# Gathering the V rows of a mixture of experts by token instead of by slot, one tile later

## The chip, the cores and the metric

One core of a Trainium2 chip (trn2) runs the whole program. The metric is the device time of one execution in microseconds (us). The kernel before takes 4674.15 us, the median of three runs (4666.22 to 4674.29).

## What is computed

One decoder layer for 1024 prompt tokens and 64 sample tokens, all in float32. After the mixers (gated linear attention and sliding-window attention) comes the part that this case is about: each token picks 128 of 16384 single-neuron experts, 16 for each of 8 heads, takes the dot product of its normalized state with each expert's row of U, and adds up the experts' rows of V, weighted.

```python
    top_s, sel = lax.top_k(cand, PEER_TOPK)
    idx = jnp.take_along_axis(cand_idx, sel, axis=-1)
    g = jax.nn.softmax(top_s, axis=-1)
...
        ub = jnp.take(u, ib, axis=0)
        act = jax.nn.gelu(jnp.einsum('pd,ped->pe', xb, ub), approximate=False)
        vb = jnp.take(v, ib, axis=0)
        return jnp.einsum('pe,ped->pd', gb * act, vb)
...
    h = x + merged @ w_out
    h = h + peer_ffn(rmsnorm(h, norm_ffn), peer_w_q, peer_keys1, peer_keys2, peer_u, peer_v)
```

A row of U or V has 1024 numbers, 4 KB. For 1088 tokens with 128 experts each, two rows per expert, that is 1.14 GB of rows fetched by index.

## The kernel before

Three stages run one after another: `project_stage` (the projections), `mix_stage` (the two mixers and their merge) and `peer_stage` (W_out, the norm, the experts, the final norm). The change is in the last, which takes the span from about 1424 us on.

`peer_stage` works in tiles of 128 tokens, one token on each partition: tiles 0 to 7 hold the prompt, tile `LAST` = 8 the 64 sample tokens. In a tile run 8 heads; a tile and a head make a unit. Tile 0 and tile `LAST` are written out, tiles 1 to 7 run in a hardware loop. Each engine has its own program:

- POOL (L1424 to L1461) fetches. One gather is one indirect DMA: it brings, for one slot k of one head, 128 rows of 4 KB, one for each token's partition. In a unit it issues 16 gathers of U for this head and, in turn with them, 16 of V for the head before. U and V rows land in rings of 8 buffers each. Before each gather it waits until its buffer was used (`u_used`, `v_used`). In tile `LAST` the 64 tokens stand on the partitions twice, and each gather brings two slots (`expert_pair`), so that a head takes 8 gathers.
- DVE (L1553 to L1709) does for each U row buffer one dot product with the normalized state (`u_dots`, L1625), then `select` for the unit two further on (L1587: the top 16 of 128 keys twice, then of 256 sums, and the experts' numbers), then `weights` of its own unit. At heads 4 and 5 it adds the residual of the next tile (`residual`), before head 6 it takes part in its norm (`norm`), after the dots of head 7 it copies the next tile's state (`take`).
- ACT (L1464 to L1550) applies Gelu to a head's dots and Exp to its scores, and makes for each slot a 128 x 128 matrix with the 128 tokens' weights on its diagonal (`diagonals`, L1493, a ring of 8).
- PE (L1712 to L1816) multiplies each diagonal with the slot's V rows, in two halves of 512 columns, into one accumulator `o_ps` of 128 x 1024, over all heads of the tile (`v_sum`, L1768). `carry` starts that sum from the residual. Between the V sums stand the queries and scores of the unit two further on, W_out of the next tile, and at head 6 the transposes of the next tile's state. A float32 matmul shows in the profile as two instructions.
- SP loads x and the mixers' result for each tile and stores the output.

`g` of the reference is `e_top` times `e_rec`; `expert` holds the numbers of the rows. The waits are on counting semaphores; an engine runs its program in order and stands at each wait.

Of the kernel before, what the change touches and what calls it, by code (L numbers as in the profile page):

```python
# [22 lines left out]
U32 = mybir.dt.uint32  # L23
# [1207 lines left out]
def peer_stage(nc, sem, x_dram, m_dram, wo_dram, wq_dram, keys_dram, u_dram, v_dram, g_ffn_dram, g_final_dram, y_dram):  # L1231
# [6 lines left out]
    U_RING, V_RING = 8, 8  # L1238
    IDX = 4
    WQ_PARTS = 2  # L1240
    DIAGS = 8
    W_OUT = {2: (0,), 3: (1,), 4: (2, 3)}
    RESIDUAL = (4, 5)
    with ExitStack() as ctx:
# [17 lines left out]


        room = sb("e_room", [P, D])
        xn_next = y = room
        mT = room[:, :].rearrange("p (k n) -> p k n", k=KT)
        xn = sb("e_xn", [P, D])
# [14 lines left out]
        picked = sb("e_picked", [P, 2, TOPK])  # L1282
        expert = sb("e_expert", [P, IDX, TOPK], U32)
        expert_pair = sb("e_expert_pair", [P, IDX, TOPK // 2], U32)
        neg_best = sb("e_neg_best", [P, IDX])
# [3 lines left out]
        dots = sb("e_dots", [P, 2, TOPK])  # L1289
        gelus = sb("e_gelus", [P, 2, TOPK])  # L1290
        weight = sb("e_weight", [P, 2, TOPK])
        diag = sb("e_diag", [P, DIAGS, P])
# [17 lines left out]
        h_used = sem("e_h_used")  # L1310
        moved = sem("e_moved")
# [11 lines left out]
        paired = sem("e_paired")  # L1323
# [7 lines left out]
        diag_ready = sem("e_diag_ready")  # L1331
        acc_ready = sem("e_acc_ready")
# [6 lines left out]
        tick = sem("tick")  # L1339
        pstep = sem("e_pstep")  # L1340
        block = ctx.enter_context(nc.Block())
        LAST = TILES

        def rows(t):
            return NSAMP if isinstance(t, int) and t == LAST else P

        def slots(t, h=0):

            return TOPK // 2 if isinstance(t, int) and t == LAST and h >= 0 else TOPK

        def slots_before(unit):

            if isinstance(unit, int) and unit > LAST * HEADS:
                return LAST * HEADS * TOPK + (unit - LAST * HEADS) * (TOPK // 2)
            return unit * TOPK

        def rounds(unit, k, ring):

            if isinstance(unit, int):
                return slots_before(unit) // ring + k // ring + 1  # L1360
            return unit * (TOPK // ring) + k // ring + 1

        @block.sync
        def _(sp):

            def load_merge(t):
                wait_alone(sp, moved, t, tick)
                wait_alone(sp, xnT_ps, 2 * t, tick)
# [8 lines left out]
            def store(t):  # L1377
                wait_alone(sp, y_ready, t + 1, tick)
                sp.dma_start(y_dram[bass.ds(t * P, rows(t)), :], y[0:rows(t), :]).then_inc(y_stored, 16)
# [536 lines left out]
```

## Time and profile before

| | |
|---|---|
| median of the runs | 4674.15 us (4666.22 to 4674.29) |
| span of the profiled execution | 4664.4 us |
| PE busy | 3850.8 us, 83% of the span |
| DVE busy | 2478.5 us, 53% |
| POOL busy | 2471.3 us, 53% |
| ACT busy | 1078.6 us, 23% |
| gathered by POOL's queue | 1143.22 MB |
| mean granted clock of TensorE | 0.910 |

The span runs from the first to the last instruction of one execution. A busy time counts the union of an engine's instructions; an engine that is busy for a large share need not be the one that the others wait for. POOL's busy time on a gather is the time in which it makes the transfer's descriptors; the data land some microseconds later. "issue" is time in which an engine waited for nothing that the profile shows.

### The profile page before, as it was taken

Reading aid. Unit: us, or ns where it says so; the run is one execution under the profiler, and the core shown is the slowest. Engines: PE = TensorE matmul, PEld = TensorE weight load, DVE = VectorE, ACT = ScalarE, POOL = GpSimd, SP = SyncE. Lnnn points to the kernel's source line nnn. Section 1 sums busy time; section 2 is a strip of 40 time slices with the busy share of each in tenths; the row PEclk is TensorE's granted clock in tenths of the full one; section 3 lists DMA queues with packets and bytes.
Section 4 is the critical chain, followed back from the end, with each engine's and each line's share of the span. In section 5 each row is a group of like instructions: output and inputs, shape, how many; then the busy total and the mean of one; then the engine's idle time right before and its main releaser. Section 6 shows DMA issues by size and latency. Waiting matters only on the chain.

```text
span 4664.4 us, 46976 instructions
## 1 busy us (share of the span) xinstructions
PE 3850.8 (83%) x13480; PEld 2174.6 (47%) x13480; DVE 2478.5 (53%) x6136; ACT 1078.6 (23%) x2482; POOL 2471.3 (53%) x2212
## 2 busy tenths in 40 slices
PE   8999997899884878787887787787788787878787
PEld 7888885555442334343343343343334343434332
DVE  3111004655434666666666666666666666666665
ACT  4221113333210212212222212222222121212221
POOL 0000000000002777777777777777777777777766
PEclk9999997999967999898999898989898999898989
DMA  3222214221136999999999999999999999999988
GB/s 135 89 85 99 77 41 155 75 65 46 53 100 252 369 379 350 385 368 362 368 375 371 367 382 363 360 373 361 358 389 352 363 374 364 346 374 358 361 322 309
DMA packets 393667, 1291.38 MB, mean 277 GB/s; under 512 B 48440, under 2 KB 84536, under 8 KB 391368
## 3 DMA queue, kind: packets, MB, share of 16 engines
q0 software_dynamic: 313920, 1143.22, 65.1%
q1 hardware_dynamic: 61080, 116.93, 7.4%
q10 hardware_dynamic: 18432, 28.42, 1.7%
q8 instruction: 109, 1.79, 0.2%
q14 instruction: 126, 1.03, 0.1%
HBM read 1243.87 MB, written 45.71 MB: 276 GB/s over the span
## 4 chain that ended last, share of the span: by engine, by line
PE 30%; DVE 14%; DMA 12%; issue 8%; POOL 3%; ACT 2%; POOLq 0%; ACTq 0%; DVEq 0%; SPq 0%
PE e_o_ps L1776 24%; DMA e_u_rows<-in_u,e_expert 8%; PE e_q_ps L1744 4%; DMA e_v_rows<-in_v,e_expert 3%; POOL e_v_rows L1429 2%; POOL e_u_rows L1429 1%; DVE e_pairs L1583 1%; DVE e_pairs L1608 1%; DVE e_top_idx L1585 1%; DVE e_top_idx L1582 1%; DVE e_pairs L1612 1%; DVE e_picked L1614 1%; DVE e_top_val L1584 1%; DVE e_pos L1585 1%; PE e_w_ps L1731 1%
## 5 line engine op out<-in xcount | busy, mean ns | idle before, releaser
L1776 PE MATMUL e_o_ps<-e_v_rows,e_diag 128*128 128x512 f32 (+1 forms) x4352 | 2061.4, 626 | 380.7 <-ACT e_diag L1499 289.3
L1631 DVE CUSTOM_DVE_ANT_0 e_u_rows<-e_u_rows,e_xn 128x1024 f32<-128x1024 f32 x1088 | 1300.6, 1223 | 1058.0 <-DMA e_u_rows<-in_u,e_expert 974.5
L1776 PEld LDWEIGHTS e_o_ps<-e_v_rows,e_diag 128*128 128x128 f32 (+1 forms) x4352 | 828.9, 197 | 1464.2 <-issue 1375.3
L1429 POOL DMA_INDIRECT e_v_rows<-in_v,e_expert x1024 | 1177.2, 1150 | 351.1 <-issue 250.8
L1429 POOL DMA_INDIRECT e_u_rows<-in_u,e_expert x1024 | 1114.3, 1088 | 376.4 <-issue 268.7
L1499 ACT ACTIVATE e_diag<-e_ident,e_weight 128x128 f32<-128x128 f32 x1024 | 361.9, 395 | 872.9 <-PE e_o_ps L1776 869.4
L1744 PEld LDWEIGHTS e_q_ps<-e_xnT,e_wq 128*128 128x128 f32 x2304 | 307.7, 209 | 117.9 <-issue 109.2
L1744 PE MATMUL e_q_ps<-e_xnT,e_wq 128*128 128x128 f32 x2304 | 314.4, 294 | 40.3 <-issue 34.0
L578 POOL TENSOR_TENSOR p_gate<-p_gate,gn 128x1024 f32<-128x1024 f32 x8 | 18.9, 2357 | 448.9 <-DMA p_gate<-z_tok 448.9
L373 PE MATMUL j_m<-j_wh,j_xh 128*128 128x512 f32 (+1 forms) x648 | 248.0, 383 | 4.5 <-DVE j_wl L309 2.5
L374 PE MATMUL j_m<-j_wl,j_xh 128*128 128x512 f32 (+1 forms) x648 | 246.2, 380 | 0.0
L375 PE MATMUL j_m<-j_wh,j_xl 128*128 128x512 f32 (+1 forms) x648 | 245.9, 380 | 0.0
L730 POOL MEMSET m_ident<- 128x128 f32 x1 | 0.2, 204 | 457.1 <-POOLq L115 457.1
L309 DVE TENSOR_TENSOR j_wl<-j_w,j_wh 128x4096 fp32r<-128x4096 f32 (+1 forms) x13 | 55.5, 4271 | 339.1 <-ACT j_wh L223 339.1
L1491 ACT ACTIVATE e_gelus<-e_dots 128x16 f32<-128x16 f32 (+1 forms) x72 | 15.5, 215 | 952.2 <-DVE e_dots L1631 952.2
L229 ACT ACTIVATE j_stage<-j_m 128x512 f32<-128x512 f32 (+1 forms) x132 | 70.5, 534 | 506.9 <-PE j_m L375 506.8
L1484 ACT ACTIVATE e_e_top<-e_best,e_neg_best 128x16 f32<-128x16 f32 x72 | 22.1, 307 | 599.7 <-DVE e_expert L1615 599.7
L373 PE MATMUL j_m<-j_xh,j_wh 128*128 128x512 f32 (+1 forms) x432 | 152.3, 353 | 2.2 <-ACT j_stage L229 2.2
L374 PE MATMUL j_m<-j_xl,j_wh 128*128 128x512 f32 (+1 forms) x432 | 152.2, 352 | 0.0
L375 PE MATMUL j_m<-j_xh,j_wl 128*128 128x512 f32 (+1 forms) x432 | 151.7, 352 | 0.0
L1731 PE MATMUL e_w_ps<-e_wo,e_room 128*128 128x512 f32 x288 | 130.1, 601 | 16.0 <-DMA e_room<-merged 16.0
L373 PEld LDWEIGHTS j_m<-j_wh,j_xh 128*128 128x128 f32 x648 | 123.2, 190 | 29.4 <-DVE j_wl L309 2.9
(255 smaller groups left out, 3930.1 us busy)
## 6 DMA issues: line engine op xcount, KB each, us to landing
j_w<-in_w_big SPq DMA_DIRECT2D x12, 2048.0 KB, 8.1
z_tok<-j_stage ACTq DMA_DIRECT2D x64, 256.0 KB, 2.0
e_u_rows<-in_u,e_expert POOLq DMA_INDIRECT x1024, 6.3
e_v_rows<-in_v,e_expert POOLq DMA_INDIRECT x1024, 6.3
z_feat<-j_stage ACTq DMA_DIRECT2D x32, 256.0 KB, 2.0
e_wq<-in_wq SPq DMA_DIRECT2D x2, 4096.0 KB, 24.0
e_room<-merged SPq DMA_DIRECT2D x9, 512.0 KB, 6.6
e_h_next<-in_x SPq DMA_DIRECT2D x9, 512.0 KB, 9.3
```

The costliest lines, as they stand in the source:

```text
L229: act.activation(stage[0:n, slot, 0:width], m_ps[slot][0:n, 0:width], func).then_inc(staged, 1)
L309: dve.tensor_tensor(wl[:, s, 0:width], w[:, 0:width], wh[:, s, 0:width].bitcast(F32), ALU.subtract).then_inc(wl_ready, 1)
L373: pe.matmul(out, lh, rh, start=(k == 0), stop=False)
L374: pe.matmul(out, lh, rl, start=False, stop=False)
L375: last = pe.matmul(out, ll, rh, start=False, stop=(k == KT - 1))
L1429: pool.indirect_dma_start(ring[:, k % size, :], None, table, bass.IndirectOffsetOnAxis(ap=index[:, h % IDX, k:k + 1], axis=0)).then_inc(go ...
L1499: act.activation(diag[:, k % DIAGS, 0:eye.shape[1]], eye[:, :], ACT.Copy, scale=weight[:, h % 2, k:k + 1]).then_inc(diag_ready, 1)
L1585: chain.step(dve.max_index(indices[:, 8:16], values[:, 8:16], rest))
L1631: dve.tensor_tensor_reduce(u_rows[:, k % U_RING, :], u_rows[:, k % U_RING, :], xn[:, :], 1.0, 0.0, ALU.mult, ALU.add, dots[:, h % 2, k:k + ...
L1731: last = pe.matmul(w_ps[:, c * BANK:(c + 1) * BANK], mT[:, k, :], wo[:, k, c * BANK:(c + 1) * BANK], start=(k == 0), stop=(k == KT - 1))
L1744: last = pe.matmul(q_ps[:, half, :], wq[:, k, j * P:(j + 1) * P], xnT[:, k, :], start=(k == 0), stop=(k == KT - 1))
L1776: last = pe.matmul(o_ps[0:n, c * BANK:(c + 1) * BANK], diag[:, k % DIAGS, 0:n], v_rows[:, k % V_RING, c * BANK:(c + 1) * BANK], start=Fals ...
```

## The change

The V rows are fetched the other way round. A gather now brings, for one token, the rows of all its 128 experts, one on each partition. For that the experts' numbers of a whole tile are collected in `expert_f`, transposed by PE and copied by DVE (`turn_experts`), which is possible only when all 8 heads of the tile are selected; so the V rows of tile t are fetched during tile t + 1, a gather of U and one of V in turn as before. In tile `LAST` two V gathers follow each U gather, and after it come the 64 V gathers of tile `LAST` itself.

The weights of a tile are collected too (`dots`, `gate`, `weights`), transposed (`turn_weights`) and put by ACT, four tokens at a time, into a column of a window that is zero elsewhere (`place`). PE takes a token's V rows with 32 columns of that window, so that the token's sum falls on its own partition within a group of 32; the tokens j, 32 + j, 64 + j and 96 + j go to the four column groups (`quad`). A quad frees its four buffers at once.

The residual no longer goes through PE; SP keeps it in DRAM (`h_dram`), loads it again two tiles later, and DVE adds the sum to it (`out_sum`). The ring of U has 7 buffers instead of 8, the state is kept for two tiles instead of being copied, the hardware loops of this stage are written out, and before the stage all semaphores of the stages before it are cleared behind a barrier (`reset`).

```diff
-    U_RING, V_RING = 8, 8
...
+    U_RING, V_RING = 7, 8
     IDX = 4
     WQ_PARTS = 2
-    DIAGS = 8
+    QUADS = 32
+    WIN = 64
     W_OUT = {2: (0,), 3: (1,), 4: (2, 3)}
     RESIDUAL = (4, 5)
...
+        xn = sb("e_xn", [P, 2, D])
...
+        window = sb("e_window", [P, 2, 4, WIN])
...
+        def lanes(t):
+            return 4 if t < LAST else 2
+        def v_at(t, j, g):
+            return t * P + lanes(t) * j + g
...
+            def load_h(t):
+                sp.wait_ge(wo_done, 2 * min(t + 3, LAST + 1))
+                wait(sp, y_stored, 16 * t)
+                sp.wait_ge(h_stored, 16 * (t + 1))
+                sp.dma_start(room[0:rows(t), :], h_dram[t, 0:rows(t), :]).then_inc(h_back, 16)
...
+            def u_gather(t, h, k):
+                i = u_at(t, h, k)
...
+            def v_gather(t, n):
+                j, g = divmod(n, lanes(t))
+                i = v_at(t, j, g)
+                wait(pool, v_used, quad_of(i - V_RING) + 1)
+                token = 32 * g + j
+                pool.indirect_dma_start(v_rows[:, i % V_RING, :], None, v_dram,
+                                        bass.IndirectOffsetOnAxis(ap=expert_T[:, t % 2, token:token + 1], axis=0)
+                                        ).then_inc(v_got[i % V_RING], 16)
...
+            for t in range(LAST + 1):
                 for h in range(HEADS):
...
+                    pool.wait_ge(picked_ready, t * HEADS + h + 1)
+                    if t and h == 0:
+                        pool.wait_ge(iT_ready, t)
+                    for k in range(slots(t)):
+                        u_gather(t, h, k)
+                        if t:
+                            per = TOPK // slots(t)
+                            for n in range(per):
+                                v_gather(t - 1, h * TOPK + per * k + n)
+            pool.wait_ge(iT_ready, LAST + 1)
+            for n in range(NSAMP):
+                v_gather(LAST, n)
...
-            def diagonals(t, h):
-                unit = t * HEADS + h
-                act.wait_ge(w_ready, unit + 1)
-                eye = ident if slots(t, h) == TOPK else ident_pair
-                for k in range(slots(t, h)):
-                    wait(act, v_used, slots_before(unit) + k - DIAGS + 1)
-                    act.activation(diag[:, k % DIAGS, 0:eye.shape[1]], eye[:, :], ACT.Copy,
-                                   scale=weight[:, h % 2, k:k + 1]).then_inc(diag_ready, 1)
...
+            def place(t, j):
+                q = t * QUADS + j
+                wait(act, v_used, q - 1)
+                n = lanes(t)
+                act.activation(window[:, q % 2, 0:n, 31], weight_T[:, j:j + 32 * (n - 1) + 1:32], ACT.Copy
+                               ).then_inc(window_ready, 1)
...
-            def take(t):
-                dve.wait_ge(xn_ready, t + 1)
-                wait(dve, u_used, t * HEADS * TOPK)
-                dve.tensor_copy(xn[:, :], xn_next[:, :]).then_inc(moved, 1)
-                dve.wait_ge(moved, t + 1)
...
+                at = slice(h * TOPK, (h + 1) * TOPK)
+                wait(dve, iT_ps, t - 1)
+                chain.link(dve.scalar_tensor_tensor(out=expert_f[:, t % 2, at], in0=picked[:, 0, :], scalar=float(NKEYS),
+                                                    in1=picked[:, 1, :], op0=ALU.mult, op1=ALU.add))
+                if t < LAST:
+                    dve.tensor_copy(expert[:, b, :], expert_f[:, t % 2, at]).then_inc(picked_ready, 1)
+                else:
+                    e = expert_f[:, t % 2, at]
+                    chain.step(dve.tensor_copy(expert_pair[0:NSAMP, b, :], e[0:NSAMP, 0:TOPK:2]))
+                    dve.tensor_copy(expert_pair[NSAMP:P, b, :], e[NSAMP:P, 1:TOPK:2]).then_inc(picked_ready, 1)
...
+            def weights(t):
+                dve.wait_ge(gelu_done, t + 1)
+                wait(dve, wT_ps, t)
+                chain.settle()
+                if t < LAST:
+                    dve.tensor_tensor(weight[:, :], dots[:, t % 2, :], gate[:, t % 2, :], ALU.mult).then_inc(w_ready, 1)
...
+            def turn_experts(t):
+                dve.wait_ge(iT_ps, t + 1)
+                dve.tensor_copy(expert_T[:, t % 2, :], t_ps[0].rearrange("p a n -> p (a n)")[:, 0:P]).then_inc(iT_ready, 1)
+            def out_sum(t):
+                n = rows(t)
+                dve.wait_ge(v_used, (t + 1) * QUADS)
+                dve.wait_ge(h_back, 16 * (t + 1))
+                dve.tensor_tensor(room[0:n, :], room[0:n, :], o_ps[0:n, :], ALU.add).then_inc(summed, 1)
...
+                    for k in range(slots(t)):
+                        dot(t, h, k)
+                        if h == 0 and k == 2 and t:
+                            weights(t - 1)
+                        if h == 0 and k == 4 and t >= 2:
+                            out_sum(t - 2)
+                        if h == 0 and k == 6 and t >= 2:
+                            out_mean(t - 2)
+                        if h == 1 and k == 0 and t >= 2:
+                            out_norm(t - 2)
+                    if unit + 2 < UNITS:
+                        select(unit + 2)
+                    gates(unit)
+                    if h == HEADS - 1:
+                        turn_experts(t)
                 chain.restart()
...
+                wait(pe, iT_ready, t - 1)
+                wait(pe, wT_ready, t - 1)
...
-            def carry(t):
-                n = rows(t)
-                wait(pe, acc_ready, t)
+            def turn_weights(t):
+                pe.wait_ge(w_ready, t + 1)
+                pe.wait_ge(xnT_ready, 2 * min(t + 2, LAST + 1))
+                out = t_ps[1].rearrange("p a n -> p (a n)")[:, 0:rows(t)]
...
+            def turn_experts(t):
+                pe.wait_ge(picked_ready, (t + 1) * HEADS)
+                pe.wait_ge(xnT_ready, 2 * min(t + 2, LAST + 1))
+                pe.transpose(t_ps[0].rearrange("p a n -> p (a n)")[:, 0:P], expert_f[:, t % 2, :], ident[:, :]
+                             ).then_inc(iT_ps, 1)
...
-                for k in range(part * count // 4, (part + 1) * count // 4):
-                    pe.wait_ge(diag_ready, slots_before(unit) + k + 1)
-                    pe.wait_ge(v_got[k % V_RING], 16 * rounds(unit, k, V_RING))
-                    for c in range(D // BANK):
-                        last = pe.matmul(o_ps[0:n, c * BANK:(c + 1) * BANK], diag[:, k % DIAGS, 0:n],
-                                         v_rows[:, k % V_RING, c * BANK:(c + 1) * BANK],
-                                         start=False, stop=(h % HEADS == HEADS - 1 and k == count - 1))
-                    last.then_inc(v_used, 1)
...
+            def quad(t, j):
+                n, q = lanes(t), t * QUADS + j
+                pe.wait_ge(window_ready, q + 1)
+                if j == 0:
+                    wait(pe, summed, t)
+                for g in range(n):
+                    i = v_at(t, j, g)
+                    pe.wait_ge(v_got[i % V_RING], 16 * (i // V_RING + 1))
                 for c in range(D // BANK):
...
+                    for g in range(n):
+                        last = pe.matmul(o_ps[32 * g:32 * g + 32, c * BANK:(c + 1) * BANK],
+                                         window[:, q % 2, g, 31 - j:63 - j],
+                                         v_rows[:, v_at(t, j, g) % V_RING, c * BANK:(c + 1) * BANK],
+                                         start=(j == 0), stop=(j == QUADS - 1))
+                last.then_inc(v_used, 1)
...
+                            quad(t - 1, 4 * h + part)
+                    if h == HEADS - 1:
+                        turn_experts(t)
+            turn_weights(LAST)
+            for j in range(QUADS):
...
+        def reset():
+            with nc.Block() as block:
+                @block.sync
+                def _(sp):
+                    for used in named.values():
+                        sp.sem_clear(used)
+            free.extend(named.values())
+            named.clear()
...
```

## Rows read from the trace of the kernel before

**Rows 1.** Page: busy us, share, instructions of each engine.

```profile
PE 3850.8 (83%) x13480; PEld 2174.6 (47%) x13480; DVE 2478.5 (53%) x6136; ACT 1078.6 (23%) x2482; POOL 2471.3 (53%) x2212
```

**Rows 2.** Page: chain that ended last, by engine and line.

```profile
PE e_o_ps L1776 24%; DMA e_u_rows<-in_u,e_expert 8%; PE e_q_ps L1744 4%; DMA e_v_rows<-in_v,e_expert 3%; POOL e_v_rows L1429 2%; POOL e_u_rows L1429 1%; DVE e_pairs L1583 1%; DVE e_pairs L1608 1%; DVE e_top_idx L1585 1%; DVE e_top_idx L1582 1%; DVE e_pairs L1612 1%; DVE e_picked L1614 1%; DVE e_top_val L1584 1%; DVE e_pos L1585 1%; PE e_w_ps L1731 1%
```

**Rows 3.** Page: costliest groups; count, busy us, mean ns, idle before.

```profile
L1429 POOL DMA_INDIRECT e_v_rows<-in_v,e_expert x1024 | 1177.2, 1150 | 351.1 <-issue 250.8
```

**Rows 4.** Waits, 1500 to 4664 us: total us, times, longest us.

```profile
DVE e_u_rows L1631 <- DMA e_u_rows<-in_u,e_expert: 974.5, 575, 6.6
...
PE e_t_ps L1719 <- DVE e_room L1569: 97.7, 8, 12.3
...
POOL e_v_rows L1429 <- PE e_o_ps L1776: 77.6, 200, 4.6
```

**Rows 5.** Timeline, POOL, 1470 to 1520: start, us, what, idle before.

```profile
1489.97 1.98 POOL L1429 DMA_INDIRECT e_u_rows<-in_u,e_expert  x1 [0.30 <-issue]
...
1496.85 0.94 POOL L1429 DMA_INDIRECT e_u_rows<-in_u,e_expert  x1 [0.30 <-issue]
```

**Rows 6.** Timeline, DVE, 1485 to 1522: five dot products.

```profile
1485.33 1.23 DVE L1631 CUSTOM_DVE_ANT_0 e_u_rows<-e_u_rows,e_xn 128x1024 f32<-128x1024 f32 x1
...
1489.92 1.22 DVE L1631 CUSTOM_DVE_ANT_0 e_u_rows<-e_u_rows,e_xn 128x1024 f32<-128x1024 f32 x1
...
1494.50 1.22 DVE L1631 CUSTOM_DVE_ANT_0 e_u_rows<-e_u_rows,e_xn 128x1024 f32<-128x1024 f32 x1
...
1507.48 1.23 DVE L1631 CUSTOM_DVE_ANT_0 e_u_rows<-e_u_rows,e_xn 128x1024 f32<-128x1024 f32 x1 [0.61 <-DMA e_u_rows<-in_u,e_expert]
...
1518.78 1.21 DVE L1631 CUSTOM_DVE_ANT_0 e_u_rows<-e_u_rows,e_xn 128x1024 f32<-128x1024 f32 x1
```

**Rows 7.** Windows by tile: us, POOL busy (x), PEclk, DMA, GB/s.

```profile
1476.60:1822.60 346.00, 269.59 (x241) 0.87 0.97 364
...
2191.70:2557.30 365.60, 279.14 (x257) 0.90 0.98 372
...
4436.80:4664.40 227.60, 158.19 (x136) 0.90 0.87 317
sum 3187.80, POOL 2441.09; mean POOL 271.23
```

**Rows 8.** Window of 10 us: all engines busy (x), PEclk, DMA, GB/s.

```profile
2510.00:2520.00 10.00, 10.00 (x24) 4.37 (x23) 5.78 (x17) 1.50 (x2) 7.56 (x9) 1.00 1.03 410
```

**Rows 9.** Timelines, POOL and DVE, around the end of a tile.

```profile
2554.32 0.94 POOL L1429 DMA_INDIRECT e_u_rows<-in_u,e_expert  x1 [0.30 <-issue]
...
2560.41 1.23 DVE L1631 CUSTOM_DVE_ANT_0 e_u_rows<-e_u_rows,e_xn 128x1024 f32<-128x1024 f32 x1 [1.32 <-DMA e_u_rows<-in_u,e_expert]
2561.56 0.08 DVE L1631 DVE_READ_ACCUMULATOR2_ANT e_dots<- 128x1 f32 x1
...
2562.50 0.42 DVE L1591 COPY e_s_sb<-e_s_ps 128x256 f32<-128x256 f32 x1
...
2572.31 0.24 DVE L1643 SCALAR_TENSOR_TENSOR e_weight<-e_gelus,e_e_rec,e_e_top 128x16 f32<-128x16 f32 x1
```

**Rows 10.** Timeline, all engines, end of the span.

```profile
4643.57 12.18 PE L1776 MATMUL e_o_ps<-e_v_rows,e_diag 128*64 128x512 f32 x28
...
4644.82 0.94 POOL L1429 DMA_INDIRECT e_v_rows<-in_v,e_expert_pair  x1 [0.30 <-issue]
```

**Rows 11.** Timeline, POOL, start of the last tile.

```profile
4436.81 0.94 POOL L1429 DMA_INDIRECT e_u_rows<-in_u,e_expert_pair  x1 [6.08 <-DVE e_expert_pair L1623]
```

**Rows 12.** Tile e_v_rows: ns min/median/max and forms; landing of its DMAs.

```profile
L1776 PE MATMUL e_o_ps<-e_v_rows,e_diag x4352: 592/592/1222, 1519.3 to 4655.2; 128*128 128x512 f32 x187, 128*64 128x512 f32 x11
...
DMA to landing us min/median/max: 4.1/6.3/10.5
```

**Rows 13.** Timelines: last dot of a burst (DVE); half a query (PE).

```profile
2493.98 1.22 DVE L1631 CUSTOM_DVE_ANT_0 e_u_rows<-e_u_rows,e_xn 128x1024 f32<-128x1024 f32 x1
...
2521.74 1.95 PE L1744 MATMUL e_q_ps<-e_xnT,e_wq 128*128 128x128 f32 x16
```

More of the change, by code:

```diff
@@ L1516, in out_root @@
                 act.activation(stat[0:rows(t), 6:7], stat[0:rows(t), 5:6], ACT.Sqrt).then_inc(out_rt, 1)
-            act.wait_ge(made, 3)
+            act.wait_ge(made, 4)
             norm(0)
+            transposed(0)
             queries(0)
             queries(1)
-            exponentials(0, 0)
-            exponentials(1, 1)
-            def tile(t):
-                first = isinstance(t, int) and t == 0
-                last = isinstance(t, int) and t == LAST
+            exponentials(0)
@@ L1528, in tile @@
+            exponentials(1)
+            for t in range(LAST + 1):
                 for h in range(HEADS):
                     unit = t * HEADS + h
-                    if h == 1 and not first:
-                        out_root(t - 1)
-                    if h == HEADS - 2 and not last:
-                        norm(t + 1)
-                    if not (first and h == 0):
-                        diagonals(t, h - 1)
-                    if h < HEADS - 2 or not last:
-                        queries(unit + 2)
@@ L1538, in tile @@
-                    gelu(t, h)
-                    if h < HEADS - 2 or not last:
-                        exponentials(unit + 2, (h + 2) % HEADS)
-                    if h == 0 and not first:
-                        evacuate(t - 1)
-            tile(0)
-            with act.Fori(1, LAST) as t:
-                tile(t)
-            tile(LAST)
-            diagonals(LAST, HEADS - 1)
-            evacuate(LAST)
+                    if t and h == 0:
+                        gelu(t - 1)
+                        weights_turned(t - 1)
+                        place(t - 1, 0)
+                        place(t - 1, 1)
@@ new lines, in _ @@
+                    if t >= 2 and h == 0:
+                        out_square(t - 2)
+                        out_root(t - 2)
+                    if h == HEADS - 2 and t < LAST:
+                        norm(t + 1)
+                        transposed(t + 1)
+                    for part in range(4):
+                        j = 4 * h + part + 2
+                        if t and j < QUADS:
+                            place(t - 1, j)
+                        if part == 1 and unit + 2 < UNITS:
+                            queries(unit + 2)
@@ L1734, in w_out, with query @@
                     last.then_inc(wo_done, 1)
-            def query(unit, h, t, half):
-                if isinstance(unit, int) and unit < HEADS:
+            def query(unit, half):
+                t, h = divmod(unit, HEADS)
+                if unit < HEADS:
                     pe.wait_ge(wq_in[h * WQ_PARTS // HEADS], 16)
@@ L1782, in _ @@
+            pe.wait_ge(made, 4)
             for part in range(4):
```

342 lines of the change are left out of this document (151 added, 191 removed).

## The prediction, made before the changed kernel ran

> **What bounds the kernel now.** I read the page first and distrust its first answer. PE is the busiest engine (83% of the span) [rows 1], the chain of waits names its V matmuls as the largest share (24%) [rows 2], and this change takes exactly those matmuls apart. But the changed stage only runs from about 1424 us on, and there three engines form a ring (POOL fetches, DVE and PE consume), so the question is who really waits for whom.
>
> Next the groups and the waits. POOL issues 2176 gathers: for V 1024 of the full tiles [rows 3] and 64 of the last, and as many for U, one for each of the 1088 dots. Its waits for PE are small: the largest such row is 77.6 us over 200 gathers [rows 4], of which most is the 0.30 us that stands before every gather anyway, with and without a releaser [rows 5]. So POOL is hardly ever stopped by a full ring, and still DVE stands waiting for U rows for 974.5 us [rows 4]. POOL paces the stage: from 1822.6 to 4436.8 us [rows 7] it issues 7 x 256 + 8 = 1800 gathers, 1.45 us each.
>
> The timeline says what the 1.45 us are. An unhindered gather takes 0.94 us plus the 0.30 us gap: 1.25 us. The gather at 1489.97 took 1.98 us [rows 5]: a dot product of DVE had started at 1489.92 and ended at 1491.14 [rows 6], and the gather ended 0.81 us after that. The gather at 1496.85 started while no dot ran (the burst's last began at 1494.50) and took 0.94 us. A gather that starts under a dot is held until the dot ends. Over the whole, POOL's busy time in the stage is 2441 us [rows 7] for 2176 gathers, 1.12 us each; that is 0.18 us over 0.94, or 0.35 us for each of the 1088 dots. PE has no part in any of it.
>
> The DMA engines look full too (share 0.97), but in a 10 us window in which gathers came at 1.25 us they moved 410 GB/s [rows 8], against 372 in the tile around it [rows 7]; 524 KB at 410 GB/s is 1.28 us. So they have a tenth in hand. The Trainium skill, page "DMA: Bandwidth & Descriptors", section "Bandwidth", puts HBM at about 358 GB/s for a core when both cores of a pair stream; by that figure, as an estimate, 1143 MB of gathers need 3193 us and no change of order could save anything. The 410 GB/s row speaks against it for this single core.
>
> **The change, part by part.** Counted from the first gather at 1476.60 us, the stage now takes 3187.8 us [rows 7].
>
> PE and ACT. 1088 diagonals go, and PE's V work is packed four at a time: per gather it is now four instructions of about 0.43 us (28 in 12.18 us [rows 10]), 1.7 us. A quad is 16 instructions: 1.7 us if the four groups run side by side, 7 if not. Neither engine paces the stage, so I cost their relief at nothing, in the middle of the stage. Cover: the V ring. Two quads fit in 8 buffers. From a quad's last gather to the next use of its buffers lie five V steps of 2.9 us, 14.5 us; landing 6.3 us [rows 12], PE 2 us, 0.8 us back to POOL: 9 us. Slack 5 us. At a tile's first quad PE also waits for DVE to add up the tile before, behind the fifth dot, 21 us after POOL's restart; its buffers are wanted at 23, so it costs about nothing, and with that wait stand only queries behind it.
>
> Tile 0 alone. V comes a tile later, so tile 0 fetches 128 U rows and nothing beside them, and DVE sets the pace. The row for this is the first head, which in the kernel before also has only U gathers: its first dot is at 1485.33, the next head's at 1518.78 [rows 6], 33.45 us. Tile 0: 8.7 + 7 x 33.45 + 23.4 (to the end of the last dot) = 266, plus 6 for the next tile's residual and norm: 272 us. Bounds: 8 heads of DVE work without any waiting, 16 x 1.15 + 10.3, give 230; POOL at 2.3 us for every gather gives 380. Now it is 346 us for 240 gathers.
>
> The tile boundary. POOL waits for the transposed experts before the first gather, U or V, of each tile. DVE makes them at the very end of its head 7, behind the last dot, the selection and the gates. Queued behind the wait on POOL is everything. A U row fetched as the last ends its dot about 7.2 us after its issue (2554.32 to 2561.63 [rows 9]); selection and gates take 10.1 us (2562.50 to 2572.55 [rows 9]), plus about 0.4 for a link and a cast more, 0.3 for the copy, 0.9 for semaphores: 19.0 us. POOL would have gone on at +2.9. Stall 16.1 us, at the ends of tiles 1 to 7: 113 us. After tile 0 it costs 11.7 us behind the last dot; before the tail, with no selection there and PE the last, 8 us. In the stalls three dots per tile hold no gather: -7 us. Bound from below: if the last rows are back faster (landing 4.1 instead of 6.3 us), 14 us each.
>
> The rings. U_RING goes from 8 to 7. After a long DVE turn nine dots ran back to back, the last at 2493.98 [rows 13]: the ring had been full, and one buffer less stops POOL one pair earlier, 2.5 us; at two heads per tile 4 us in sum, 7 x 4 = 28 us. In head 6 PE stands at the transposes for the norm, 12 us per tile now [rows 4]. The old ring (23 us deep) hid that; with quads it overruns the slack by some 4 us, partly at the same moment: 11 us in all. Together 39, bounds 0 and 100.
>
> The last tile. 64 U and 128 V gathers: 192 x 1.25 + 64 x 0.35 = 262, plus 10 because V now comes twice as often and the slack of its ring is gone: 272. What goes is the wait for the paired experts, 6.08 us, 5.8 over the gap [rows 11]. Then 64 V gathers with no dots and nothing beside them, a tail that did not exist (it was 8): 64 x 1.30 = 83. End: 19.6 us from the last gather now, of which PE's queue is 4 (last issue 4644.82, PE done at 4655.75 [rows 10], landing 6.3 us after the issue by 4651); with an addition of 1.2 more and without the queue, 17.
>
> Between the stages all semaphores are cleared one by one behind a further barrier, about a hundred. No row shows it. The shortest instruction in my rows, a read of an accumulator, takes 0.08 us [rows 9]; a hundred of those are 8 us, and the other bound is nothing, if the clears overlap. I take 6, barrier included.
>
> **Sum.** Tiles 1 to 7: 1792 x 1.449 (2614.2 less 5.8, over 1800) = 2597, + 113 - 7 + 39 = 2742. All: 272 + 12 + 2742 + 272 + 8 + 83 + 17 = 3406, against 3187.8: +218, with the clears +224. The profiled execution has a span of 4664.4, the median of the runs is 4674.2, 9.8 above it; I add the difference to the median: 4898 us, 4.8% slower. In short: same number of gathers at the same price, but 128 at the front and 64 at the back no longer share their time with the other table, and POOL stops at every tile.
>
> **Rivals.** (1) The column groups run one after another. For: a 64-column V matmul takes 592 ns like the 128-column one [rows 12]; nothing in this trace shows two side by side. The Trainium skill, page "TensorE: Matmul & The Clock Gate", Part 3, says they overlap (three column groups 2.38x); by it this rival falls. Price: a ring cycle of 8.7 + 6.3 + 7.8 + 0.8 = 23.6 us against 23.2, and up to 25.5 with a query half (1.95 us [rows 13]) in front: 112 cycles, 45 to 260 us; last tile and tail another 110. 5050 to 5265, about 5140. Chance 11%.
>
> (2) Faster: the gathers miss the dots. The 0.20 us over 1.25 are a matter of phase: had gathers started between dots, the pace would fall to the 1.28 us of the DMA engines. Then 1792 x 0.17 + 15 = 320 us go: 4578. It decides against my sign below 1.33 us per gather. For: the rhythm of both engines is newly set each tile. Against: DVE still does one dot per pair of gathers, started by a landing, and every tile now runs at 1.43 to 1.5. Chance 8%.
>
> (3) Both rings together stop POOL more often than counted, 100 to 150 us: 5020. Chance 6%.
>
> Forecast 75%, 4800 to 4990 by its bounds. What is left out of 4790 to 5050 is (2), and most of (1). Within 0.2%, about what a measurement here can tell from no change, only a partial (2) lands. Faster by more 0.08, within 0.03, slower 0.89.
>
> **What would show it.** Right: tile 0 near 272 us with few POOL instructions; 1.45 us per gather inside tiles; a hole of 15 to 17 us in POOL at each boundary released by DVE; a POOL tail of 83 us without dots; PE's share of the stage far down at no gain. Wrong: a pace under 1.35 (rival 2); POOL waiting for PE for more than 50 us outside the boundaries and quads of 7 us (rival 1); boundaries under 10 us.

## The result: 3.9% slower

The changed kernel takes 4843.03 us, the median of four runs (4839.03 to 4856.17); the kernel before took 4670.18 us beside it. The ratio is 1.0392, with a 95% interval of 1.0364 to 1.0421. The forecast was 4898 us in a range of 4790 to 5050. The profiled executions have spans of 4838.0 and 4664.4 us, 173.6 us apart, and that difference is what the readings below account for.

From the page of the changed kernel: the span, the busy times of the engines, and the groups of the dots, of PE's V matmuls and of the two kinds of gathers (they answer rows 1 and 3).

```profile
span 4838.0 us, 39968 instructions
...
PE 2788.1 (58%) x13463; PEld 1570.0 (32%) x13463; DVE 2498.6 (52%) x6140; ACT 591.9 (12%) x1502; POOL 2456.2 (51%) x2213
...
L1643 DVE CUSTOM_DVE_ANT_0 e_u_rows<-e_u_rows,e_xn 128x1024 f32<-128x1024 f32 x1088 | 1306.7, 1223 | 1147.7 <-DMA e_u_rows<-in_u,e_expert 1002.6
L1798 PE MATMUL e_o_ps<-e_v_rows,e_window 128*32 128x512 f32 x4352 | 916.1, 955 | 1381.2 <-DMA e_v_rows<-in_v,e_expert_T 1357.7
L1442 POOL DMA_INDIRECT e_u_rows<-in_u,e_expert x1024 | 1149.7, 1123 | 555.5 <-issue 417.0
L1451 POOL DMA_INDIRECT e_v_rows<-in_v,e_expert_T x1088 | 1207.3, 1110 | 374.0 <-issue 312.3
```

PE gave up more than 1000 us of busy time and the kernel became slower. The gathers of U and V last 1123 and 1110 ns on average, where V had 1150 [rows 3]: the same instruction at about the same price.

The windows by tile, which answer rows 7 (stretch, its length, POOL busy and its instructions, granted clock, DMA share, GB/s): tile 0, tile 2, tile 7, the last tile up to the end of its U gathers, and the tail.

```profile
1483.80:1767.70 283.90, 170.76 (x128) 0.60 0.71 242
...
2156.50:2533.10 376.60, 277.40 (x256) 0.66 0.95 364
...
4062.10:4443.20 381.10, 282.23 (x256) 0.69 0.95 358
4443.20:4736.50 293.30, 210.08 (x193) 0.65 0.92 347
4736.50:4838.00 101.50, 61.18 (x64) 0.90 0.90 341
```

Tile 0 has 128 gathers in 283.9 us, where the kernel before had 241 in 346. A full tile takes 376 to 389 us for 256 gathers, of which 16 us are the hole at its end. The tail of 64 V gathers is there with its ending, 101.5 us.

The timeline around such a hole, POOL, DVE and PE, answers rows 9. The columns are start, duration, what, and the idle time before it.

```profile
2516.39 1.13 POOL L1451 DMA_INDIRECT e_v_rows<-in_v,e_expert_T  x1 [0.30 <-issue]
...
2520.91 1.23 DVE L1643 CUSTOM_DVE_ANT_0 e_u_rows<-e_u_rows,e_xn 128x1024 f32<-128x1024 f32 x1 [1.65 <-DMA e_u_rows<-in_u,e_expert]
...
2525.83 0.14 PEld L1785 LDWEIGHTS e_t_ps<-e_ident,e_expert_f 128*128 128x128 f32 x1 [1.66 <-issue]
...
2531.92 0.23 DVE L1636 TENSOR_SCALAR e_gate<-e_e_top,e_e_rec 128x16 f32<-128x16 f32 x1
2532.06 0.28 DVE L1662 CAST e_expert_T<-e_t_ps 128x128 uint32<-128x128 f32 x1
...
2533.11 0.94 POOL L1442 DMA_INDIRECT e_u_rows<-in_u,e_expert  x1 [15.58 <-issue]
```

POOL issues its last gather of tile 2 at 2516.39. The last dot ends at 2522.1, the selection and the gates at 2532.2. PE had transposed the experts at 2525.83 already, 6 us before DVE came to copy them. The next gather starts at 2533.11, after 15.58 us of idleness. The eight holes of this kind are 15.3 to 16.6 us long. POOL's row names no releaser for them ("issue"); that it waits for the copy is read from the times: in all eight the gather starts 0.76 us after the copy ends. A ninth hole, of 9.2 us, stands before the tail.

The waits of POOL over tiles 1 to 7 (total us, times, longest), which answer the POOL row of rows 4:

```profile
POOL e_u_rows L1442 <- DVE e_dots L1643: 27.0, 8, 5.0
POOL e_v_rows L1451 <- PE e_o_ps L1798: 22.1, 35, 2.0
```

With the 0.30 us that stand before every gather taken off, POOL's rings cost it 36 us in all seven tiles. Counted the same way they cost 48 us in the kernel before, so they cost no more than there.

The matmuls of one quad, from PE's timeline, and the form row of their tile, which answers rows 12:

```profile
2627.54 3.64 PE L1798 MATMUL e_o_ps<-e_v_rows,e_window 128*32 128x512 f32 x16 [6.59 <-DMA e_v_rows<-in_v,e_expert_T]
```

```profile
L1798 PE MATMUL e_o_ps<-e_v_rows,e_window x4352: 589/1061/1065, 1784.3 to 4829.7; 128*32 128x512 f32 x198
```

Sixteen instructions of 1061 ns take 3.64 us together. How many run side by side shows best in a quad at the upper of TensorE's two levels (2.4 GHz), where an instruction takes 592 ns in both kernels:

```profile
2182.88 1.92 PE L1798 MATMUL e_o_ps<-e_v_rows,e_window 128*32 128x512 f32 x16 [2.67 <-DMA e_v_rows<-in_v,e_expert_T]
```

That is 0.12 us for each of the sixteen, where the kernel before took 0.435 us for each (28 in 12.18 us [rows 10]). So four run side by side, and in the trace the four of a group start within 0.04 us of each other.

Most quads run at the lower level (1.2 GHz), as the median of 1061 ns says. The granted clock was 0.69 over tile 3, where PE was busy for 171 of 380 us; in the same tile of the kernel before it was 0.91, with PE busy for 295 of 367 us.

Put together, from these windows and the first gather of each tile:

| where | us |
|---|---|
| first gather at 1483.8 instead of 1476.6 | +7 |
| tile 0: 268 us without its hole, for 128 gathers, which at 1.449 us each are 185 | +83 |
| eight holes | +126 |
| 1792 gathers of tiles 1 to 7 at 1.432 instead of 1.449 us | -31 |
| last 256 gathers (379 us, the ninth hole within), against 256 x 1.449 | +8 |
| the end behind the last gather, 15.7 instead of 19.6 | -4 |
| the waits of the kernel before in its last tile | -15 |
| sum | +174 |

### The profile page after: what moved, and what is told of

It reads as the page before. It is cut to its first block and busy times, and to the rows that moved or that the text cites. A ratio compares the mean times of both kernels' runs of the same rounds, so it can differ in the third digit from the quotient of the medians.

```text
span 4838.0 us, 39968 instructions
## 1 busy us (share of the span) xinstructions
PE 2788.1 (58%) x13463; PEld 1570.0 (32%) x13463; DVE 2498.6 (52%) x6140; ACT 591.9 (12%) x1502; POOL 2456.2 (51%) x2213
## 5 line engine op out<-in xcount | busy, mean ns | idle before, releaser
L1798 PE MATMUL e_o_ps<-e_v_rows,e_window 128*32 128x512 f32 x4352 | 916.1, 955 | 1381.2 <-DMA e_v_rows<-in_v,e_expert_T 1357.7
L1442 POOL DMA_INDIRECT e_u_rows<-in_u,e_expert x1024 | 1149.7, 1123 | 555.5 <-issue 417.0
L1451 POOL DMA_INDIRECT e_v_rows<-in_v,e_expert_T x1088 | 1207.3, 1110 | 374.0 <-issue 312.3
L1798 PEld LDWEIGHTS e_o_ps<-e_v_rows,e_window 128*32 128x32 f32 x4352 | 182.2, 148 | 1852.7 <-issue 1811.3
L1757 PEld LDWEIGHTS e_q_ps<-e_xnT,e_wq 128*128 128x128 f32 x2304 | 330.3, 229 | 167.5 <-issue 158.8
L1757 PE MATMUL e_q_ps<-e_xnT,e_wq 128*128 128x128 f32 x2304 | 354.3, 318 | 6.3 <-ACT e_xnT L1487 6.3
L1515 ACT ACTIVATE e_window<-e_weight_T 128x4 f32<-128x4 f32 (+1 forms) x288 | 59.2, 209 | 2147.3 <-PE e_o_ps L1798 2147.0
L1769 PE MATMUL e_s_ps<-e_keys,e_q_sb 128*128 128x128 f32 x288 | 67.8, 372 | 201.6 <-ACT e_q_sb L1492 201.6
L1769 PEld LDWEIGHTS e_s_ps<-e_keys,e_q_sb 128*128 128x128 f32 x288 | 50.7, 249 | 297.0 <-ACT e_q_sb L1492 297.0
L797 DVE TENSOR_SCALAR rel<-b 128x128 f32<-128x128 f32 x256 | 52.9, 280 | 158.3 <-DMA v<-z_tok 158.3
```

The source lines that it names most:

```text
L1442: pool.indirect_dma_start(u_rows[:, i % U_RING, :], None, u_dram, bass.IndirectOffsetOnAxis(ap=index[:, h % IDX, k:k + 1], axis=0)).then_i ...
L1451: pool.indirect_dma_start(v_rows[:, i % V_RING, :], None, v_dram, bass.IndirectOffsetOnAxis(ap=expert_T[:, t % 2, token:token + 1], axis=0 ...
L1515: act.activation(window[:, q % 2, 0:n, 31], weight_T[:, j:j + 32 * (n - 1) + 1:32], ACT.Copy).then_inc(window_ready, 1)
L1757: last = pe.matmul(q_ps[:, half, :], wq[:, k, j * P:(j + 1) * P], xnT[:, k, :], start=(k == 0), stop=(k == KT - 1))
L1769: last = pe.matmul(s_ps[:, half, :], q_sb[:, half, :], keys[:, 2 * h + half, :], start=True, stop=True)
L1798: last = pe.matmul(o_ps[32 * g:32 * g + 32, c * BANK:(c + 1) * BANK], window[:, q % 2, g, 31 - j:63 - j], v_rows[:, v_at(t, j, g) % V_RING ...
```

## The experiments

The theory was that POOL sets the pace of the stage in both kernels, that its gathers are long because dots of DVE hold them, that PE's work is covered, and that the change loses by tile 0 and by the holes. The rivals were that the DMA engines (share 0.97) or PE (83% busy) set the pace. All ratios are against the kernel before on the same chip.

**Half of PE's V work in the kernel before.** This leaves out the second half of the columns of each expert sum, but for the last slot of a tile.

```diff
-                    for c in range(D // BANK):
+                    for c in range(2 if h % HEADS == HEADS - 1 and k == count - 1 else 1):
```

> The kernel before with half of PE's V work: the second half of the 1024 columns is summed for the last slot of each tile alone, so half of each expert sum is left out; gathers, diagonals and waits stay. Theory (POOL sets the pace, PE is covered): within 0.3% of the kernel before, 4660 to 4680 us, PE's busy share down by some 900 us of work. Rival (PE is the bound, as its 83% and the chain say): at least 100 us faster.

Measured: 4665.43 us, ratio 1.0003 (0.9986 to 1.002). PE's share of the span fell from 83 to 72% and nothing moved. PE did not bound the kernel before, so no relief of PE could make it faster.

**The experts turned earlier in the changed kernel.** Nothing is left out; two calls move.

```diff
                     for k in range(slots(t)):
                         dot(t, h, k)
+                        if h == HEADS - 1 and k == 2:
+                            turn_experts(t)
...
                     gates(unit)
-                    if h == HEADS - 1:
-                        turn_experts(t)
```

On PE `turn_experts(t)` moves from the end of head 7 to its start.

> The changed kernel with the experts turned earlier: PE transposes them at the start of head 7 and DVE copies them after the third dot of head 7, instead of both at the end of head 7. Theory (POOL's holes of 16 us at the eight tile boundaries are plain loss): the holes go, 8 x 16 = 128 us, less a few us given back at the rings: 4710 to 4740 us. Rival (the holes only let a backlog of the DMA engines drain, so part comes back elsewhere): less than 60 us gained, over 4780 us.

Measured: 4727.73 us, 115 us less than the changed kernel and 1.0138 (1.0114 to 1.0163) against the kernel before. Its windows by tile:

```profile
1485.50:1749.40 263.90, 164.07 (x128) 0.61 0.74 257
2117.30:2488.30 371.00, 285.95 (x256) 0.69 0.98 370
2853.70:3228.20 374.50, 291.19 (x256) 0.67 0.98 366
```

These are tiles 0, 2 and 4. The hole behind tile 0 is gone (263.9 for 283.9 us), and the full tiles take 365 to 376 us, as in the kernel before. The ninth hole, before the tail, went too. The spans differ by 113 us: of the 135 us of all nine holes, 22 did not come back, because between the holes the changed kernel had been a little quicker (1.432 us a gather, here 1.446). So most of the holes was loss and not a backlog being worked off. What is left against the kernel before, 60 us, is 78 us in tile 0 and 9 us at the start, less the 15 us of waits that the kernel before has in its last tile and some 12 us elsewhere.

**The state in PSUM.** The dot reads a U row and the state. Here the state lies in PSUM. Two banks are freed for it, which needs two changes of waits.

```diff
-        xn = sb("e_xn", [P, D])
+        xn = pb("e_xn", [P, D])
...
-        q_ps = pb("e_q_ps", [P, 2, P])
-        s_ps = pb("e_s_ps", [P, 2, NKEYS])
-        t_ps = [pb(f"e_t_ps{i}", [P, 4, P]) for i in range(2)]
+        qs_ps = pb("e_qs_ps", [P, 4, P])
+        q_ps, s_ps = qs_ps[:, 0:2, :], qs_ps[:, 2:4, :]
+        t_one = pb("e_t_ps", [P, 4, P])
+        t_ps = [t_one, t_one]
...
-                    wait(pe, xnT_ready, 2 * (t - 1) + i + 1)
+                    wait(pe, xnT_ready, 2 * t + i)
...
                 wait(pe, q_ready, unit)
+                wait(pe, s_taken, unit)
```

> The kernel before with the state that the dots multiply by (e_xn) in two PSUM banks instead of SBUF; to free them, queries and scores share a bank and the two transposes share one. Theory (a gather is held while a dot reads both operands from SBUF): gathers take 0.95 us each also under a dot, their mean falls from 1.12 to under 1.0, and 2176 gathers x 0.17 us = up to 370 us go until the DMA engines (1.28 us a gather) or the rings bind: 4380 to 4480 us. Rival (the DMA engines set the pace, and POOL's long gathers are back-pressure): unchanged, 4660 to 4700 us, the same mean duration of a gather.

Measured: 4475.62 us, ratio 0.9597 (0.9574 to 0.962). The groups of the dots and the gathers on its page:

```profile
L1632 DVE CUSTOM_DVE_ANT_0 e_u_rows<-e_u_rows,e_xn 128x1024 f32<-128x1024 f32 x1088 | 1293.3, 1218 | 861.3 <-DMA e_u_rows<-in_u,e_expert 798.0
...
L1430 POOL DMA_INDIRECT e_v_rows<-in_v,e_expert x1024 | 978.4, 955 | 439.1 <-issue 253.5
L1430 POOL DMA_INDIRECT e_u_rows<-in_u,e_expert x1024 | 968.9, 946 | 447.8 <-issue 241.9
```

The mean V gather fell from 1150 to 955 ns, and the dot kept its length. From the timeline of POOL and DVE, a gather that starts under a dot:

```profile
2255.92 1.22 DVE L1632 CUSTOM_DVE_ANT_0 e_u_rows<-e_u_rows,e_xn 128x1024 f32<-128x1024 f32 x1
2255.99 0.94 POOL L1430 DMA_INDIRECT e_u_rows<-in_u,e_expert  x1 [0.30 <-issue]
...
2257.06 1.22 DVE L1632 CUSTOM_DVE_ANT_0 e_u_rows<-e_u_rows,e_xn 128x1024 f32<-128x1024 f32 x1
2257.24 0.95 POOL L1430 DMA_INDIRECT e_v_rows<-in_v,e_expert  x1 [0.30 <-DVE e_dots L1632]
```

It starts 0.07 us into a dot and takes 0.94 us. In the kernel before the same meeting took 1.98 us [rows 5, 6]. Counted over both whole traces: in the kernel before 809 gathers start under a dot, last 1407 ns on average and end 0.82 us after the dot (median); here 863 do and last 944 ns. Another instruction of DVE, whose operands still lie in SBUF, still holds a gather in this trace, which also ends 0.82 us after it:

```profile
2253.58 1.28 DVE L1666 SCALAR_TENSOR_TENSOR e_room<-e_room,e_stat,e_g_final 128x1024 f32<-128x1024 f32 x1
2253.92 1.76 POOL L1430 DMA_INDIRECT e_v_rows<-in_v,e_expert  x1 [0.30 <-issue]
```

So what holds a gather is a dot whose both operands lie in SBUF. The Trainium skill, page "SBUF — State Buffer", section "Who interferes with whom", states it as a rule: a DVE instruction with two SBUF inputs contends with a GpSimd instruction that reads SBUF, and one with at most one SBUF input, outside DVE's two-port modes, does not. The two traces agree for a gather, which reads its rows' numbers from SBUF, with 1.98 and 0.94 us.

**Only the banks shared,** the state in SBUF as before: the control for the run above.

```diff
-        xn = pb("e_xn", [P, D])
+        xn = sb("e_xn", [P, D])
```

> Control for the run before it: only the sharing of banks (queries with scores, the two transposes in one), the state stays in SBUF. Both theories: 4670 to 4700 us, gathers of 1.12 us on average; what it adds over the kernel before is the price of the sharing alone.

Measured: 4670.79 us, ratio 1.0003 (0.9987 to 1.002). The sharing costs nothing, and the 4% are the place of the state alone.

**PE's V work halved again, at the quicker pace.** The same edit as in the first experiment, in the kernel with the state in PSUM; the same half of the sums is left out.

```diff
-                    for c in range(D // BANK):
+                    for c in range(2 if h % HEADS == HEADS - 1 and k == count - 1 else 1):
```

> The first run's kernel (state in PSUM, otherwise as before) with half of PE's V work, as in the third run: the second half of the columns is left out of the sums but for one slot a tile. At 1.45 us a gather this made no difference. Now gathers come at 1.31 us and POOL stands 25 us a tile at full rings, half of it in rows released by PE. Theory (at the quicker pace PE's V work begins to count): 60 to 130 us below that kernel's 4476, so 4345 to 4415 us, with POOL's stops under 10 us a tile. Rival (the stops come from DVE's long turns, or the DMA engines are full at 1.28 us): under 30 us gained.

Measured: 4451.76 us, ratio 0.9526 (0.9499 to 0.9553), 24 us less by the medians. The theory missed and the rival was right. Tile 2 without and with the cut:

```profile
2146.90:2495.20 348.30, 243.80 (x256) 0.92 0.99 391
```

```profile
2142.30:2490.00 347.70, 244.21 (x257) 0.76 0.99 391
```

The tile stays at 348 us. POOL's stops, which I had put down to PE by their releasers, are the same 26 us a tile with half of PE's work gone: something behind them sets the 348. The two profiled executions differ by 17 us, mostly in tile 1, in the last tile and behind the last gather.

**The changed kernel with both,** the early turn and the state in PSUM, and DVE copying it there once a tile. The banks are shared as in the other kernels with the state in PSUM; the diff shows the copy and the dot alone.

```diff
+            def take(t):
+                dve.wait_ge(xn_ready, t + 1)
+                wait(dve, u_used, u_at(t, 0, 0))
+                chain.link(dve.tensor_copy(xp[:, :], xn[:, t % 2, :]))
...
-                dve.tensor_tensor_reduce(u_rows[:, i % U_RING, :], u_rows[:, i % U_RING, :], xn[:, t % 2, :], 1.0, 0.0,
+                dve.tensor_tensor_reduce(u_rows[:, i % U_RING, :], u_rows[:, i % U_RING, :], xp[:, :], 1.0, 0.0,
```

> The changed kernel with the early turn of the experts (fourth run) and the state in PSUM (first run; DVE copies it there from SBUF once a tile). Theory: gathers of 0.95 us throughout, 1.25 to 1.30 us apart. Tile 0 264 us, tiles 1 to 7 at 256 x 1.30 = 333 us each, the rest 192 x 1.30 + 64 x 1.34 + 20: 1485 + 264 + 2331 + 250 + 86 + 20 = 4436 span, about 4445 us, so the relief of PE now pays for tile 0: 10 to 50 us below the first run's 4476. Rival (V landings of 8 us and quads together leave the V ring of 8 no slack at this pace): POOL stops at V, 340 to 350 us a tile, 4490 to 4560 us.

Measured: 4532.51 us, ratio 0.97 (0.9672 to 0.9727). The theory's 4445 us missed: it is slower than the kernel before with the state in PSUM. The rival's ranges hold both the time and the tile, but not for its reason, since the kernel without quads has the same tile. Tiles 0 and 2:

```profile
1489.90:1721.50 231.60, 121.00 (x129) 0.63 0.78 289
2066.00:2414.80 348.80, 243.04 (x257) 0.67 1.00 393
```

The full tile takes 348.8 us, again the same. Tile 0 takes 231.6 us for 128 gathers, where half a full tile would be 174: of the 62 us between this span and that of the kernel before with the state in PSUM, this is 57.

**The same with 8 buffers for U,** and one buffer for the state in SBUF instead of two.

```diff
-    U_RING, V_RING = 7, 8
+    U_RING, V_RING = 8, 8
...
-        xn = sb("e_xn", [P, 2, D])
+        xn_one = sb("e_xn", [P, D])
+        xn = xn_one[:, :].rearrange("p (a n) -> p a n", a=1)
```

> The same with one buffer of the state in SBUF instead of two, and 8 buffers for U instead of 7. If the ring of U costs what I forecast for the change (about 4 us a tile, 28 us in all), this is 20 to 40 us faster than the kernel with 7. If the ring of U has slack, as the short gaps of the changed kernel suggest (5 us a tile, as many as before), the two are equal within 0.2%, and the forecast's ring term was too large.

Measured: 4522.73 us, ratio 0.968 (0.9652 to 0.9707), 0.2% below the one with 7.

```profile
1480.90:1705.80 224.90, 121.42 (x129) 0.64 0.80 298
2050.90:2399.10 348.20, 243.79 (x257) 0.70 0.99 393
```

The full tile is the same, 348.2 us; 7 us are gained in tile 0, where DVE draws on the ring alone. Another 9 us between the two profiled executions stand ahead of the first gather (1480.9 for 1489.9 us), where no ring plays a part. So at this pace the eighth buffer is worth 7 us at most, and nothing in a full tile. At the pace of the changed kernel it was not tried.

**A quarter of the bytes left out, state in PSUM.** The V gathers bring 2 KB a row, and the sums run over these 512 columns (and read other rows than the reference, since the index then counts half rows).

```diff
-                pool.indirect_dma_start(ring[:, k % size, :], None, table,
+                width = BANK if table is v_dram else D
+                pool.indirect_dma_start(ring[:, k % size, 0:width], None, table.rearrange("e (a n) -> (e a) n", n=width),
```

> The first run's kernel (state in PSUM) whose V gathers bring 2 KB of each row instead of 4, and whose sums run over these 512 columns alone: a quarter of the gathered bytes is left out. All kernels with the state in PSUM ran their full tiles in 348 us, 1.36 us a gather, whatever their rings and their PE work. Theory (that is the pace of the DMA engines at 4 KB): the tile falls towards POOL's own 256 x 1.25 = 320 us, so 325 to 335 us, and the whole by 110 to 180 us, to 4300 to 4365. Rival (the rings and DVE's turns set the 348): 340 to 348 us a tile, over 4400 us.

Measured: 4339.24 us, ratio 0.9285 (0.9262 to 0.9309).

```profile
2118.30:2451.40 333.10, 246.03 (x257) 0.79 0.90 307
```

The tile fell to 333 us, 1.30 us a gather, towards POOL's own 1.25. So the 348 us, 1.36 us a gather, hang on the bytes: 256 x 524 KB in 348 us are 386 GB/s. They are no steady pace, though. Three stretches of 10 us from tile 2 with all the bytes (state in PSUM, PE's work whole):

```profile
2150.00:2160.00 10.00, 7.56 (x9) 1.00 1.03 408
2320.00:2330.00 10.00, 7.56 (x9) 1.00 1.03 411
2430.00:2440.00 10.00, 3.02 (x4) 0.85 0.45 147
```

In 29 of the tile's 35 stretches the DMA engines moved 405 to 412 GB/s, which is one gather in 1.28 us. The other six lie where POOL had stopped at a full ring for 6.5, 4.6 and 6.8 us (before its gathers at 2173, 2219 and 2436 us), and they lose some 16 us. So a full tile is the transfers at 1.28 us a gather, about 332 us, and gaps behind POOL's stops. With fewer bytes these stops fell from 26 to 9 us a tile. Which part a larger ring would give back was not tried.

**The same cut in the kernel before,** state in SBUF.

> The same cut (2 KB of each V row, sums over 512 columns) in the kernel before, with the state in SBUF. Theory (gathers held by dots set its pace, not the DMA engines): a tile stays at 365 to 375 us although a quarter of the bytes is gone, 4640 to 4680 us in all, the mean gather still 1.10 to 1.13 us. Rival (the DMA engines, whose share is 0.97, set its pace too): at least 100 us faster.

Measured: 4745.05 us, ratio 1.0147 (1.0124 to 1.017). Neither theory had this: with a quarter of the bytes gone the kernel is slower. One full tile, and the groups of the gathers:

```profile
2214.90:2592.30 377.40, 298.29 (x257) 0.71 0.84 271
```

```profile
L1430 POOL DMA_INDIRECT e_u_rows<-in_u,e_expert x1024 | 1270.5, 1241 | 362.9 <-issue 281.8
L1430 POOL DMA_INDIRECT e_v_rows<-in_v,e_expert x1024 | 1146.6, 1120 | 318.4 <-issue 283.7
```

The DMA engines were not the bound, since less to move did not help. The mean U gather rose from 1088 to 1241 ns, and the tile from 366 to 377 us. The U rows land sooner (median 5.3 us after the issue, 6.3 before), so the dots start at another moment between the gathers. They hold hardly more of them, 822 against 809 over the whole trace, but each for longer: 1541 ns on average against 1407, with the same 0.82 us behind the dot, so these gathers start earlier under their dots. That accounts for the longer gathers; that the landings are what moved the moment is argued, not shown by a run that shifts it alone.

## Why the prediction was right, point by point

**What bounds.** Right in every part that was tested. POOL sets the pace, a dot holds a gather that starts under it, PE is covered. The size came out 50 us too high (224 forecast, 173.6 measured): tiles 1 to 7 took 66 us less than forecast (39 of it the rings, 24 the pace, 3 the holes), the last tile 16 us more.

**The pace.** Taken as unchanged, 1.449 us a gather; it was 1.432 in tiles 1 to 7, 31 us less in all. Some 21 us of this are shorter gathers (1.107 us on average, 1.119 before), of which my 7 us for dots that run in the holes are a part; some 10 us are fewer stops at the rings. The run without holes had 1.446 and gathers of 1.119 us, so most of the gain came with the holes.

**Tile 0.** Forecast 284 us with its hole, from one row of the first head; measured 283.9. It is no luck of the total: the last dot ends 273.0 us after the first gather (272 forecast), the heads take 33.1 to 34.3 us but for one of 37.6 (33.45 forecast), and DVE is busy for 238 of the 284 us. No run changed what stands in tile 0, so its 83 us are read from the windows and not taken away by an experiment. The upper bound of 380 us does not follow from its own words (128 gathers at 2.3 us are 294).

**The boundary.** Forecast 16.1 us, measured 15.3 to 16.6, ended by DVE's copy, with PE ready 6 us earlier. (The 7.2 us in its sum are 7.3 by rows 9, as its total of 19.0 has it.)

**The rings.** The term that was mis-sized: 39 us for U_RING 7 and the transposes in head 6. POOL's waits for its rings in tiles 1 to 7 are 36 us in the changed kernel against some 48 before, so nothing was added in sum. The stops moved, though: in head 6 each tile now has one of 2.5 to 5.0 us before a U gather and one of 1.0 to 2.0 before a V gather, where it had one before a V gather (3.3 to 4.6, once 6.7), so the smaller ring may have cost something there. I had found one pair of rows with the ring full and multiplied it by two heads a tile; the other stops of the kernel before stood in the heads at a tile's start, where the hole now stands instead.

**The last tile.** Forecast 272 + 8 + 83 = 363 us, measured 379 (284.1 + 9.2 + 85.8). Here the wait that I had dismissed came through: PE's first quad waits for DVE to add up the tile before, behind the fifth dot. The rows of all engines there:

```profile
4466.08 1.23 DVE L1643 CUSTOM_DVE_ANT_0 e_u_rows<-e_u_rows,e_xn 128x1024 f32<-128x1024 f32 x1 [2.94 <-DMA e_u_rows<-in_u,e_expert_pair]
...
4467.23 1.22 DVE L1668 TENSOR_TENSOR e_room<-e_room,e_o_ps 128x1024 f32<-128x1024 f32 x1
...
4468.55 3.31 PE L1798 MATMUL e_o_ps<-e_v_rows,e_window 128*32 128x512 f32 x16 [5.64 <-issue]
...
4472.16 0.94 POOL L1451 DMA_INDIRECT e_v_rows<-in_v,e_expert_T  x1 [11.34 <-PE e_o_ps L1798]
```

In a full tile the sum is ready before the V ring is full. With two V gathers behind each U gather the ring is full earlier, and POOL stood 11.34 us. I had costed that wait for the full tiles and not for the last. The 10 us that I put there for the lost slack cover part of it: POOL's stops in the tile are 16 us, and the other 7 us of the miss are longer gathers.

**The start.** Forecast 6 us, from no row; measured 7.2 us at the first gather. Kernels with the same front differ there by up to 4 us (first gather at 1476.6 to 1480.9 us in the runs with the code of before), so this says little. The clearing shows better as the distance from the last store of the stage before to the first load of this one, 10.8 us where it was 4.6 (1419.19 to 1423.75 us in the trace of before):

```profile
1420.13 1.35 SPq L1073 DMA_DIRECT2D merged<-n_mT  x2
1430.94 0.62 SPq L1392 DMA_DIRECT2D e_wo<-in_wo  x1
```

**The words behind the sum.** I wrote that 128 gathers at the front and 64 at the back lose by standing alone. The sum did not say so, and the trace does not: in a stage where POOL issues one gather after another, the tail's 64 at 1.36 us are no dearer than others. Only the front loses, because there DVE cannot use what POOL could fetch.

**The rivals.** The column groups do run side by side, against rival 1. Rival 2 was priced with a floor of 1.28 us a gather, from a 10 us window. The transfers do run at it for longer, but over a full tile no kernel here got below 1.36 with all its bytes, so the tenth that the DMA engines had in hand was worth a twentieth. At 1.36 the changed kernel could have gained 160 us on its pace and, by my sum, still been slower, so the sign was safer than 8% said. And the pace can move the other way, as the last experiment shows. Rival 3 did not come.

## What to carry to other kernels

Before relieving the busiest engine, ask whom the pacing engine waits for: here it waited for hardly anybody (48 us of 2614), and halving PE's V work changed nothing. When a step is moved a tile later, look for what then runs alone at the front and for the one value that the pacing engine needs at each boundary; produce it as soon as its inputs are there, not at the end of a long turn (115 us here). Where GpSimd issues gathers beside DVE instructions with two SBUF operands, put one operand into PSUM: that alone made the kernel before 4% faster, and it is the fastest full version of this study, 4475.62 us.

## What the runs showed of the hardware that was not expected

- A gather of 128 rows of 4 KB costs POOL 0.94 us and a gap of 0.30 us; under a dot with two SBUF operands it ends 0.82 us after the dot (median of 809). The transfers of such gathers run at up to 408 to 412 GB/s, one in 1.28 us, also over 28 of them in a row at the end of the changed kernel, where no dots run:

```profile
4783.00:4818.00 35.00, 25.55 (x28) 1.00 1.03 408
```

Over a whole tile with both tables 1.36 us a gather was reached, 386 GB/s.
- Fewer bytes can cost time: 4745 against 4673 us when a quarter was left out. POOL's stops at the rings nearly vanished (5 us in tiles 1 to 7, 48 before), and its gathers grew by more than that, from 1.119 to 1.182 us on average.
- PE with less to do ran at a lower clock. Halving its V work in the kernel before, and nothing else, took the granted clock of the run from 0.91 to 0.79. A 128x512 V matmul took 592 ns [rows 12] in the kernel before and a 32-column one mostly 1061 ns in the changed one, so that a quad took up to 3.64 us where I had expected 2. It stayed covered.
